# Decoder block on one core: gate slabs of the attention re-placed, statistics by quarters, merged tiles awaited one by one

## The chip, the cores and the metric

The kernel runs on one core of a Trainium2 chip. The metric is the time of the device for one execution, in microseconds. TensorE does the matmuls and the transposes, VectorE (DVE) and ScalarE (ACT) the element-wise work, GpSimd (POOL) the gathers, and SyncE (SP) issues most of the loads.

## The reference

One decoder layer on 512 tokens and 16 meta tokens of width 1024, in float32. Cut to the stages that the change touches:

```python
z = h @ w_in + b_in                      # q, k, v of both mixers, forget gate, gates ga and gb
oa = sliding_window_attention(...)       # 8 heads, window of 128, sinks, relative bias
ob = forgetting_attention(...)           # 8 heads, causal over all tokens, decayed
merged = sigmoid(ga) * (oa @ w_pa) + sigmoid(gb) * (ob @ w_pb)
y = merged @ w_o
h = layer_norm(DEEPNORM_ALPHA * h + y, ln1_g, ln1_b)
y = peer_ffn(h, ...)                     # top 16 of 16384 one-neuron experts for each of 8 heads
out = layer_norm(DEEPNORM_ALPHA * h + y, ln2_g, ln2_b)
```

## The kernel before

All large products are made slab by slab. A slab is 128 x 1024 numbers of a weight, eight tiles of 128 x 128. SyncE loads it into a ring of four (`load`), ScalarE rounds it to a high part (`split_hi`, L451), VectorE subtracts that and gets the low part (`split_lo`, L455), and TensorE makes of each tile three matmuls: high times low, low times high, high times high (`split_product`, L464 to L466). The splits run three slabs ahead of TensorE (`AHEAD`). With 512 tokens a tile is so three matmuls of 512 columns and a slab 24. Everything is float32 in parts, and each engine runs its own program in order; counters (semaphores) tie them together.

The stages, in order: 19 projection slabs; the attention, with gate slabs between; the `mix` slabs, one for each of the eight 128-row tiles m of the merged result; eight output slabs (`w_o`); the layer norm; 16 query slabs and the key scores; 128 slabs of `u_exp` and 128 of `v_exp`, beside which POOL gathers rows and VectorE uses them.

**The attention** has 64 units, a unit being one head of one block of 128 queries: 32 of the sliding window, in pairs, that is steps 0 to 15, and 32 of the forgetting attention, one a step, steps 16 to 47. Eight units are a block result; the blocks w = 0 to 7 end with steps 3, 7, 11, 15, 23, 31, 39 and 47. TensorE's iteration s issues the scores of step s + 1 (L1432), then the gate tiles that `TILES[s]` gives to this step, then the transposes of the probabilities of step s - 1 (L1453, L1456), then the products with the values of step s - 2 (L1475, L1478) into bank `psO[w % 2]`. VectorE adds bias and mask, takes the maximum (L942), inverts the sum and scales the probabilities `pexp` of step s - 1 (L951). ScalarE takes the exponentials (L614) and evacuates the transposes (L627, L630). Three iterations after a block ended, ScalarE takes its high part out of `psO` (`oT_hi`, L638) and VectorE, in the same iteration of its own loop, its low part (`oT_lo`, L960). The scores of step s stand in `psS[s % 2]`; in the last eight steps (40 to 47) a row has 528 columns, 16 of which lie in the second half, which else holds the result of the gate slabs.

**The gate slabs** are the columns ga and gb of `w_in`, two for each m. 14 of the 16 (`N_GATE`) are made in the attention, tile by tile as `TILES` says (16 steps of four tiles, 16 of two, then 3, 3, 2, 2, 2, 2, 2, 0, and none in the last eight steps), and ScalarE moves each result with its bias to `gate_input(v)` (L620). The two gates of m = 7 are made as whole slabs in the merge, ahead of the last `mix` slab.

**The merge.** For each m, TensorE makes the two products of `oT` into two of the banks 4 to 7, ScalarE has taken the sigmoid of the two gates (L648, L655), VectorE multiplies and adds (`mix`, L973, L975), and ScalarE and VectorE split the result (`m_hi` L658, `m_lo` L977). All three engines go in the same order of m.

**The output.** The eight output slabs start when all eight `m_lo` are there. VectorE makes `acc` from each (L995), and TensorE turns it behind the next slab (`turn_sum`, L1507) so that tokens are rows. Four of the turned tiles fill banks 4 to 7, 512 columns each; VectorE takes `bn_stats` of the four banks twice (`half_stats`, L984), after tile 3 and after tile 7, and the transposes of tile 4 wait for the first four. Behind the second four come `bn_aggr`, the inverse root, and a spread over the columns by small matmuls (L1527).

The lines that say what waits:

```python
                w = block_ended(s - 3)              # VectorE, attention
                if w is not None:
                    dve.wait_ge(o_hi_done, w + 1)
...
            pe.wait_ge(o_lo_done, 2 * NBLK)         # TensorE, ahead of the merge
...
                pe.wait_ge(m_lo_done, KT)           # TensorE, ahead of the output slabs
...
                if k == KT // 2:                    # TensorE, turn_sum
                    pe.wait_ge(r_stats_done, 1)
```

Of the kernel before, what the change touches and what calls it, by code (L numbers as in the profile page):

```python
# [21 lines left out]
P = 128  # L22
D = 1024
SEQ = 512
# [3 lines left out]
KT = D // P  # L28
# [20 lines left out]
N_GATE = 2 * (KT - 1)  # L49
FIRST_MIX = FIRST_MERGE + N_GATE  # L50
FIRST_OUT = FIRST_MERGE + N_MERGE
# [178 lines left out]

TILES = [4] * 16 + [2] * 16 + [3, 3, 2, 2, 2, 2, 2, 0] + [0] * 8

# [17 lines left out]
def build(nc, x, meta, consts, buckets, outside, norm_cols, b_cols, rel_bias, sinks, w_proj, w_merge, w_out,  # L250
          w_pq, subkeys, u_exp, v_exp, u_rows, norm_rows, out):
    ctx = ExitStack()
    with ctx:
# [53 lines left out]
        with ExitStack() as s:  # L307
            diag, unit_h = place(s, diag=([P, 2 * NBLK, P], F32), unit_h=([P, 2, SEQ], F32))
            stats1, mv1, rs1 = place(s, stats1=([P, NBLK, 12], F32), mv1=([P, NBLK, 2], F32), rs1=([P, 5, NBLK], F32))

# [50 lines left out]
        def out_bank(m):  # L361

            return (m + 4) % KT

        wide = [psS[:, 0, :], psS[:, 1, :], psT[:, :], psO[:, :, :].rearrange("p o q -> p (o q)")]
# [102 lines left out]
        def slab_parts(slot, k):  # L468
            return hi[:, slot, k * P:(k + 1) * P], lo[:, slot, k * P:(k + 1) * P]

        def gate_input(v):
# [102 lines left out]
        def _(act):  # L574
# [28 lines left out]
            for s in range(N_STEPS + 4):  # L603
# [13 lines left out]
                if v is not None:  # L617
                    act.wait_ge(slab_used, FIRST_MERGE + v + 1)
                    tile = N_PROJ + 8 * (v % 2) + v // 2
                    nc.scalar.activation(gate_input(v), psS[:, v % 2, SEQ:], ACT.Identity,  # L620
                                         bias=bcol[:, tile:tile + 1]).then_inc(gate_in_done, 1)
# [14 lines left out]
                if w is not None:  # L636
# [3 lines left out]
                                         ACT.Copy).then_inc(o_hi_done, 1)  # L640

            for m in range(KT):
                if m >= 2:
                    act.wait_ge(mix_done, m - 1)
                if m < KT - 1:
                    split_hi(act, FIRST_MIX + m + AHEAD)
                    for j in range(2):
                        nc.scalar.activation(gate[:, m % 2, j, :], gate_input(2 * m + j), ACT.Sigmoid).then_inc(gate_done, 1)  # L648
                else:
                    for j in range(3):  # L650
                        n = FIRST_MIX + m + j
                        split_hi(act, n + AHEAD)
                        if j < 2:
                            act.wait_ge(slab_used, n + 1)
                            nc.scalar.activation(gate[:, m % 2, j, :], psS[:, m % 2, j * SEQ:(j + 1) * SEQ], ACT.Sigmoid,  # L655
                                                 bias=bcol[:, N_PROJ + 8 * j + m:N_PROJ + 8 * j + m + 1]).then_inc(gate_done, 1)
                act.wait_ge(mix_done, m + 1)
                nc.scalar.activation(m_hi[:, m, :], mix[:, m % 2, 0, :], ACT.Copy).then_inc(m_hi_done, 1)  # L658
# [148 lines left out]
        def _(dve):  # L807
# [89 lines left out]
            dve.wait_ge(ck_in, 16)  # L897
            for s in range(N_STEPS + 4):
                last_step = 1 <= s <= N_STEPS
# [54 lines left out]
                if v is not None:  # L954
                    split_lo(dve, FIRST_MERGE + v + AHEAD)
                w = block_ended(s - 3)
                if w is not None:
# [4 lines left out]


            for m in range(KT):
                last = FIRST_MIX + m if m < KT - 1 else FIRST_OUT - 1
                for n in range(FIRST_MIX + m, last + 1):
                    split_lo(dve, n + AHEAD)
                dve.wait_ge(slab_used, last + 1)
                dve.wait_ge(gate_done, 2 * m + 2)
                if m >= 2:  # L970
                    dve.wait_ge(m_hi_done, m - 1)
                for j in range(2):
                    own.mark(V.tensor_tensor(mix[:, m % 2, j, :], banks[4 + 2 * (m % 2) + j], gate[:, m % 2, j, :], ALU.mult))  # L973
                own.settle()
                V.tensor_tensor(mix[:, m % 2, 0, :], mix[:, m % 2, 0, :], mix[:, m % 2, 1, :], ALU.add).then_inc(mix_done, 1)  # L975
                dve.wait_ge(m_hi_done, m + 1)
                V.tensor_tensor(m_lo[:, m, :], mix[:, m % 2, 0, :], m_hi[:, m, :].bitcast(F32),  # L977
                                ALU.subtract).then_inc(m_lo_done, 1)

            def half_stats(c):  # L980

                dve.wait_ge(r_turned, c + 1)
                for t in range(NBLK):
                    ins = V.bn_stats(stats1[:, t, 6 * c:6 * c + 6], banks[4 + t])  # L984
                    if t < NBLK - 1:
                        own.mark(ins)
                ins.then_inc(r_stats_done, 1)
                dve.wait_ge(r_stats_done, c + 1)

            for m in range(KT):  # L990
                split_lo(dve, FIRST_OUT + m + AHEAD)
                own.link(V.tensor_tensor(acc[:, m, :], hT_hi[:, m, 0:SEQ].bitcast(F32), hT_lo[:, m, 0:SEQ].bitcast(F32),
                                         ALU.add))
                dve.wait_ge(slab_used, FIRST_OUT + m + 1)
                V.scalar_tensor_tensor(acc[:, m, :], acc[:, m, :], ALPHA, psS[:, m % 2, 0:SEQ],  # L995
                                       ALU.mult, ALU.add).then_inc(r_done, 1)
                if m == KT // 2 + 1:
                    half_stats(0)
            half_stats(1)
            for t in range(NBLK):  # L1000
# [332 lines left out]
        def _(pe):  # L1333
# [85 lines left out]
            for s in range(-1, N_STEPS + 2):  # L1419
                r = s + 1  # L1420
                if r < N_STEPS:
                    if r >= 2:
                        pe.wait_ge(exp_done, exp_count(r - 2))
                    for u, first in placed(r):
                        window, n, h, tile, half = unit_of(u)
                        rows = slice(HD * half, HD * half + HD)
                        if width_of(u) > SEQ:
                            pe.wait_ge(gate_in_done, N_GATE - 1 + r % 2)
                        q = (qaT if window else qbT)[rows, tile, n * P:(n + 1) * P]
                        for c, k0, k1 in key_runs(u):  # L1430
                            k = kaT[rows, k0:k1] if window else kbT[rows, tile, k0:k1]
                            last = mm(psS[:, r % 2, first + c:first + c + k1 - k0], q, k, start=True, stop=True)  # L1432
                    last.then_inc(s_mm, 1)
                for done in range(tiles_before(max(s, 0)), tiles_before(s + 1)):
                    v, k = done // KT, done % KT
                    if k == 0:
                        pe.wait_ge(lo_done, FIRST_MERGE + v + 1)
                        if v >= 2:
                            pe.wait_ge(gate_in_done, v - 1)
                    last = slab(FIRST_MERGE + v, (FIRST_MERGE + v) % RING, psS[:, v % 2, SEQ:], tokens, tokens_lo,  # L1440
                                [(k, k)], ends=(k == 0, k == KT - 1))
# [17 lines left out]
                if s >= 2:  # L1459
# [20 lines left out]
                    last.then_inc(pv_mm, 1)  # L1480

            pe.wait_ge(o_lo_done, 2 * NBLK)
            for m in range(KT):
                for j in (range(3) if m == KT - 1 else (2,)):
                    n = FIRST_MIX + m + (j if m == KT - 1 else 0)
                    pe.wait_ge(lo_done, n + 1)
                    if j < 2:
                        last = slab(n, n % RING, psS[:, m % 2, j * SEQ:(j + 1) * SEQ], tokens, tokens_lo, all_k)
                    else:
                        if m >= 2:  # L1490
                            pe.wait_ge(mix_done, m - 1)
                        for e in range(2):
                            last = slab(n, n % RING, banks[4 + 2 * (m % 2) + e], lambda k: oT_hi[:, e, k, :],
                                        lambda k: oT_lo[:, e, k, :], [(4 * e + k, k) for k in range(4)])
                    last.then_inc(slab_used, 1)

# [3 lines left out]
            def turn_sum(k):  # L1500

                pe.wait_ge(r_done, k + 1)
                if k == KT // 2:
                    pe.wait_ge(r_stats_done, 1)
                for t in range(NBLK):
                    at = k % (KT // 2) * P
                    last = turn(banks[4 + t][:, at:at + P], acc[:, k, t * P:(t + 1) * P], ident)  # L1507
                if k % (KT // 2) == KT // 2 - 1:
                    last.then_inc(r_turned, 1)

            pe.wait_ge(gate_done, 2 * KT)
            for m in range(N_OUT):
                n = FIRST_OUT + m
                pe.wait_ge(lo_done, n + 1)
                pe.wait_ge(m_lo_done, KT)
                if m >= 2:
                    pe.wait_ge(r_done, m - 1)
                slab(n, n % RING, psS[:, m % 2, 0:SEQ], lambda k: m_hi[:, k, :], lambda k: m_lo[:, k, :],
                     all_k).then_inc(slab_used, 1)
                if m >= 1:  # L1520
# [211 lines left out]
```

## Time and profile before

| | us |
|---|---|
| median of 3 runs | 1705.8 |
| lowest and highest | 1704.66, 1707.39 |
| the profiled execution, its own time | 1718.52 |
| its span, first to last instruction | 1716.4 |
| TensorE busy | 1653.8 |
| VectorE busy | 1339.5 |
| ScalarE busy | 735.2 |
| GpSimd busy | 452.1 |
| mean granted clock of TensorE | 0.983 |

The profile comes from one execution, whose own time stands beside its span; the runs of the median were made without it. Times in the profile count from the first instruction. The attention lies between 149 and 360 us, the merge follows up to 417, the output slabs up to 478, and the two stages of expert slabs fill the time from 610 to 1700. A granted clock of 1.00 is TensorE's full 2.4 GHz and 0.50 is 1.2 GHz. Durations of single matmuls overlap each other, so it is the distance of their starts that tells the pace.

### The profile page before, as it was taken

The numbers are of one execution on the slowest core, as the hardware profiler recorded it, in microseconds if no ns is written. First come the engines' busy times: TensorE is split into PE (matmuls) and PEld (weight loads), VectorE is DVE, ScalarE is ACT, GpSimd is POOL, SyncE is SP. The second block draws the span as 40 slices with busy tenths as digits, with TensorE's granted clock in tenths as the row PEclk, the third lists the DMA queues.
The fourth block names the chain that finished last, engine by engine and source line by source line (L and its number), as shares of the span: only waits on it lengthen the run. The fifth ranks groups of instructions, "written<-read, shape, count | busy, mean of one in ns | idle before, by whom it ended". The sixth has DMA issues, their size and how long they took to land. (4 is left out here: it accounts for less than half of the span.)

```text
span 1716.4 us, 26821 instructions
## 1 busy us (share of the span) xinstructions
PE 1653.8 (96%) x9808; PEld 1523.3 (89%) x9808; DVE 1339.5 (78%) x2848; ACT 735.2 (43%) x1288; POOL 452.1 (26%) x314
## 2 busy tenths in 40 slices
PE   5999999999979999999999999999999999999996
PEld 4897776577768899999999999999999999999996
DVE  5434554644467888999999989967989999999898
ACT  4214544333143354566766754434333333333331
POOL 0000000000001105133132432332544545457550
PEclk9999999889989999999999999999999999999998
DMA  5731111012214459699899999999999999999991
GB/s 167 198 95 55 39 48 38 25 49 86 74 61 155 129 157 379 217 341 336 269 316 340 353 307 332 341 398 392 382 400 410 407 408 408 407 402 409 407 404 78
DMA packets 185441, 438.47 MB, mean 255 GB/s; under 512 B 17832, under 2 KB 102000, under 8 KB 182880
## 3 DMA queue, kind: packets, MB, share of 16 engines
q1 hardware_dynamic: 73872, 227.43, 36.3%
q0 software_dynamic: 44080, 161.06, 25.5%
q10 hardware_dynamic: 67360, 48.28, 8.5%
q8 instruction: 78, 1.28, 0.3%
q14 instruction: 51, 0.42, 0.1%
HBM read 380.57 MB, written 56.13 MB: 254 GB/s over the span
## 5 line engine op out<-in xcount | busy, mean ns | idle before, releaser
L464 PE MATMUL psS<-hT_lo,hi 128*128 128x368 f32 (+2 forms) x1504 | 518.4, 345 | 4.6 <-DVE hT_lo L1021 3.9
L465 PE MATMUL psS<-hT_hi,lo 128*128 128x368 f32 (+2 forms) x1504 | 510.1, 339 | 0.0
L466 PE MATMUL psS<-hT_hi,hi 128*128 128x368 f32 (+2 forms) x1504 | 508.5, 338 | 0.0
L455 DVE TENSOR_TENSOR lo<-raw,hi 128x1024 fp32r<-128x1024 f32 x323 | 394.6, 1222 | 119.7 <-ACT hi L451 110.5
L451 ACT ACTIVATE hi<-raw 128x1024 fp32r<-128x1024 f32 x323 | 340.0, 1053 | 177.4 <-PE psS L466 124.0
L569 POOL DMA_INDIRECT gat<-in_u_rows,idx x144 | 214.7, 1491 | 393.1 <-DVE gat L1195 214.8
L464 PEld LDWEIGHTS psS<-hT_lo,hi 128*128 128x128 f32 x1504 | 283.8, 189 | 30.8 <-issue 15.6
L466 PEld LDWEIGHTS psS<-hT_hi,hi 128*128 128x128 f32 x1504 | 283.9, 189 | 13.4
L465 PEld LDWEIGHTS psS<-hT_hi,lo 128*128 128x128 f32 x1504 | 283.8, 189 | 11.1
L569 POOL DMA_INDIRECT gat<-in_v_exp,idx x144 | 220.8, 1533 | 233.9 <-DVE gat L1195 151.4
L766 ACT ACTIVATE act_hi<-act_t 128x368 fp32r<-128x368 f32 x128 | 65.6, 513 | 278.9 <-DVE act_t L1246 264.0
L464 PE MATMUL psS<-act_lo,hi 128*128 128x368 f32 x512 | 169.6, 331 | 0.0
L465 PE MATMUL psS<-act_hi,lo 128*128 128x368 f32 x512 | 169.4, 331 | 0.0
L466 PE MATMUL psS<-act_hi,hi 128*128 128x368 f32 x512 | 168.9, 330 | 0.0
L1205 DVE SCALAR_TENSOR_TENSOR y_row<-gat,coef,y_row 128x1024 f32<-128x1024 f32 x128 | 164.0, 1281 | 2.6 <-DVE y_row L1205 0.5
L1195 DVE SCALAR_TENSOR_TENSOR gat<-gat,h_row 128x1024 f32<-128x1024 f32 x128 | 154.5, 1217 | 1.7 <-DMA gat<-in_u_rows,idx 1.7
L771 ACT ACTIVATE gelu<-psS 128x368 f32<-128x368 f32 x128 | 61.0, 476 | 185.5 <-PE psS L466 174.0
L556 POOL DMA_DIRECT2D sk_raw<-in_subkeys x1 | 0.5, 538 | 402.7 <-DVE acc L995 402.7
L465 PEld LDWEIGHTS psS<-act_hi,lo 128*128 128x128 f32 x512 | 96.2, 188 | 0.0
L466 PEld LDWEIGHTS psS<-act_hi,hi 128*128 128x128 f32 x512 | 96.2, 188 | 0.0
L464 PEld LDWEIGHTS psS<-act_lo,hi 128*128 128x128 f32 x512 | 96.1, 188 | 0.0
L464 PE MATMUL psT<-act_lo,hi 128*128 128x368 f32 x256 | 86.0, 336 | 3.4 <-DVE act_lo L1254 2.9
(303 smaller groups left out, 2630.1 us busy)
## 6 DMA issues: line engine op xcount, KB each, us to landing
raw<-in_u_exp SPq DMA_DIRECT2D x128, 512.0 KB
raw<-in_v_exp SPq DMA_DIRECT2D x128, 512.0 KB
gelu_dram<-gelu ACTq DMA_DIRECT2D x128, 184.0 KB
gates_dram<-gates ACTq DMA_DIRECT2D x92, 256.0 KB
gel_in<-gelu_dram SPq DMA_DIRECT2D x128, 184.0 KB
raw<-in_w_merge SPq DMA_DIRECT2D x24, 512.0 KB
gate_even<-gates_dram SPq DMA_DIRECT2D x8, 1472.0 KB
gate_odd<-gates_dram SPq DMA_DIRECT2D x8, 1472.0 KB
```

Source lines behind the costliest of these rows:

```text
L451: nc.scalar.activation(hi[:, n % RING, :], raw[:, n % RING, :], ACT.Copy).then_inc(hi_done, 1)
L455: nc.vector.tensor_tensor(lo[:, n % RING, :], raw[:, n % RING, :], hi[:, n % RING, :].bitcast(F32), ALU.subtract).then_inc(lo_done, 1)
L464: nc.tensor.matmul(out_ap, w_h, x_l, start=start, stop=False)
L465: nc.tensor.matmul(out_ap, w_l, x_h, start=False, stop=False)
L466: return nc.tensor.matmul(out_ap, w_h, x_h, start=False, stop=stop)
L556: pool.dma_start(sk_raw[:, :, :], subkeys).then_inc(keys_in, 16)
L569: nc.gpsimd.indirect_dma_start(out=gat[:, i % GATHERS, :], out_offset=None, in_=u_rows if kind == DOT else v_rows, in_offset=bass.Indirect ...
L766: nc.scalar.activation(act_hi[:, w % RING, :], act_t[:, w % RING, :], ACT.Copy).then_inc(ahi_done, 1)
L771: nc.scalar.activation(gelu[:, s % RING, :], banks[s % RING][:, 0:DENSE], ACT.Gelu).then_inc(gelu_done, 1)
L1195: V.scalar_tensor_tensor(row, row, 1.0, against, ALU.mult, ALU.mult, accum_out=dots[:, j:j + 1]).then_inc(item_done, 1)
L1205: V.scalar_tensor_tensor(total[:, :], row, coef[:, j:j + 1], total[:, :], ALU.mult, ALU.add).then_inc(item_done, 1)
```

## The change

- The splits and orders of the slabs change: all 16 gate slabs come first, then the eight `mix` slabs (`FIRST_MIX`, `w_merge`).
- `TILES`: steps 14 and 15 have three tiles instead of four, steps 32 to 39 have 2, 2, 2, 2, 1, 1, 0, 0, steps 40 to 43 none, and steps 44 to 47 two each. Slab 13 is made in these last four, in bank `psO[0]` (`gate_bank`), after a wait for the `oT_hi` and `oT_lo` of block 6, whose bank it is.
- VectorE's `oT_lo` comes four iterations after the block's end, not three; its loop is one longer.
- The gate slabs 14 and 15 (m = 7) are made as whole slabs directly behind the last attention step, into the two halves of `psS[1]`, ahead of the wait for the last `oT_lo`. ScalarE takes their sigmoids in the turn of m = 7. ScalarE and VectorE split two more slabs ahead of their loops over m.
- The first output slab waits for `m_lo` tile by tile.
- The statistics of the sums are taken by quarters: two turned tiles each, 256 columns, in banks 4 and 5, 6 and 7, 1 and 3, and 4 and 5 again (`sum_bank`); `stats1` is twice as long; VectorE takes a quarter ahead of its wait for the next output slab.

```diff
-FIRST_MIX = FIRST_MERGE + N_GATE
+FIRST_MIX = FIRST_MERGE + 2 * KT
-TILES = [4] * 16 + [2] * 16 + [3, 3, 2, 2, 2, 2, 2, 0] + [0] * 8
+TILES = [4] * 14 + [3] * 2 + [2] * 16 + [2, 2, 2, 2, 1, 1, 0, 0] + [0, 0, 0, 0, 2, 2, 2, 2]
+        def sum_bank(c, t):
+            return banks[((4, 5), (6, 7), (1, 3), (4, 5))[c][t // 2]]
+        def gate_bank(v):
+            return psS[:, v % 2, SEQ:] if v < N_GATE - 1 else psO[:, 0, :]
# ScalarE
+            for j in range(2):
+                split_hi(act, FIRST_MERGE + N_GATE + j + AHEAD)
             for m in range(KT):
                 if m >= 2:
                     act.wait_ge(mix_done, m - 1)
+                split_hi(act, FIRST_MIX + m + AHEAD)
+                for j in range(2):
+                    if m < KT - 1:
                         nc.scalar.activation(gate[:, m % 2, j, :], gate_input(2 * m + j), ACT.Sigmoid).then_inc(gate_done, 1)
+                    else:
+                        act.wait_ge(slab_used, FIRST_MERGE + N_GATE + j + 1)
+                        nc.scalar.activation(gate[:, m % 2, j, :], psS[:, 1, j * SEQ:(j + 1) * SEQ], ACT.Sigmoid,
...
# VectorE
-            for s in range(N_STEPS + 4):
+            for s in range(N_STEPS + 5):
-                w = block_ended(s - 3)
+                w = block_ended(s - 4)
+            for j in range(2):
+                split_lo(dve, FIRST_MERGE + N_GATE + j + AHEAD)
             for m in range(KT):
+                split_lo(dve, FIRST_MIX + m + AHEAD)
+                dve.wait_ge(slab_used, FIRST_MIX + m + 1)
...
+            def quarter_stats(c):
                 dve.wait_ge(r_turned, c + 1)
                 for t in range(NBLK):
+                    ins = V.bn_stats(stats1[:, t, 6 * c:6 * c + 6],
+                                     sum_bank(c, t)[:, t % 2 * (SEQ // 2):(t % 2 + 1) * (SEQ // 2)])
...
+                if m >= 3 and m % 2 == 1:
+                    quarter_stats((m - 3) // 2)
                 dve.wait_ge(slab_used, FIRST_OUT + m + 1)
                 V.scalar_tensor_tensor(acc[:, m, :], acc[:, m, :], ALPHA, psS[:, m % 2, 0:SEQ],
                                        ALU.mult, ALU.add).then_inc(r_done, 1)
-                if m == KT // 2 + 1:
-                    half_stats(0)
-            half_stats(1)
+            quarter_stats(3)
+            dve.wait_ge(r_stats_done, 4)
# TensorE
-                            pe.wait_ge(gate_in_done, N_GATE - 1 + r % 2)
+                            pe.wait_ge(gate_in_done, N_GATE - 1 - r % 2)
+                        if v == N_GATE - 1:
+                            pe.wait_ge(o_hi_done, 2 * NBLK - 1)
+                            pe.wait_ge(o_lo_done, 2 * NBLK - 1)
+            for j in range(2):
+                n = FIRST_MERGE + N_GATE + j
+                pe.wait_ge(lo_done, n + 1)
+                slab(n, n % RING, psS[:, 1, j * SEQ:(j + 1) * SEQ], tokens, tokens_lo, all_k).then_inc(slab_used, 1)
             pe.wait_ge(o_lo_done, 2 * NBLK)
             for m in range(KT):
+                n = FIRST_MIX + m
+                pe.wait_ge(lo_done, n + 1)
+                if m == 1:
+                    pe.wait_ge(gate_in_done, N_GATE)
...
-                if k == KT // 2:
+                if k == KT - 2:
                     pe.wait_ge(r_stats_done, 1)
                 for t in range(NBLK):
-                    at = k % (KT // 2) * P
-                    last = turn(banks[4 + t][:, at:at + P], acc[:, k, t * P:(t + 1) * P], ident)
-                if k % (KT // 2) == KT // 2 - 1:
+                    at = (t % 2 * 2 + k % 2) * P
+                    last = turn(sum_bank(k // 2, t)[:, at:at + P], acc[:, k, t * P:(t + 1) * P], ident)
+                if k % 2 == 1:
                     last.then_inc(r_turned, 1)
...
-                pe.wait_ge(m_lo_done, KT)
+                for k in range(KT):
+                    if m == 0:
+                        pe.wait_ge(m_lo_done, k + 1)
+                    last = slab(n, n % RING, psS[:, m % 2, 0:SEQ], lambda k: m_hi[:, k, :], lambda k: m_lo[:, k, :],
+                                [(k, k)], ends=(k == 0, k == KT - 1))
```

## Rows read from the trace of the kernel before

**Rows 1.** The page's first part: busy time of each engine.
```profile
PE 1653.8 (96%) x9808; PEld 1523.3 (89%) x9808; DVE 1339.5 (78%) x2848; ACT 735.2 (43%) x1288; POOL 452.1 (26%) x314
```

**Rows 2.** Waits of TensorE over the span: total us, times, longest us.
```profile
PE psS L464 <- DVE m_lo L977: 3.6, 1, 3.6
PE psT L1453 <- DVE pexp L951: 3.5, 4, 1.8
PE psT L1507 <- DVE stats L984: 3.3, 1, 3.3
...
PE psT L464 <- DVE oT_lo L960: 1.5, 1, 1.5
```

**Rows 3.** TensorE by stretches, late attention: length, busy us, granted clock, DMA, GB/s.
```profile
316.64:329.83 13.19, 13.19 (x73) 1.00 0.13 40
329.83:331.61 1.78, 0.00 (x1) 0.96 0.00 0
331.61:355.35 23.74, 23.74 (x82) 0.50 0.00 1
```

**Rows 4.** Timeline, iteration 42: start us, length us, instruction [idle before <-releaser].
```profile
327.97 0.57 ACT L638 ACTIVATE oT_hi<-psO 128x512 fp32r<-128x512 f32 x1
...
328.57 0.69 DVE L960 TENSOR_TENSOR oT_lo<-psO,oT_hi 128x512 fp32r<-128x512 f32 x1 [2.49 <-ACT oT_hi L638]
...
331.61 0.38 PE L1453 MATMUL psT<-cst,pexp 128*16 128x128 f32 x1 [1.78 <-DVE pexp L951]
```

**Rows 5.** Timeline, two tile-free steps at full clock.
```profile
319.51 1.25 PE L1432 MATMUL psS<-kbT,qbT 64*128 64x512 f32 x4
...
322.40 1.25 PE L1432 MATMUL psS<-kbT,qbT 64*128 64x512 f32 x4
...
323.69 0.78 DVE L934 SCALAR_TENSOR_TENSOR psS<-psS,cq,ckB 128x528 f32<-128x528 f32 x1 [0.51 <-PE psS L1432]
```

**Rows 6.** Timeline, end of the last `mix` slab: first and last of 15 matmuls.
```profile
413.61 0.40 PE L464 MATMUL psO<-oT_lo,hi 128*128 128x512 f32 x1
...
416.88 0.40 PE L466 MATMUL psO<-oT_hi,hi 128*128 128x512 f32 x1
```

**Rows 7.** TensorE by stretches around three waits behind the merge, columns as before.
```profile
417.28:420.86 3.58, 0.00 (x0) 0.91 0.07 30
420.86:427.24 6.38, 6.38 (x15) 0.52 0.25 85
459.21:462.55 3.34, 0.00 (x1) 0.79 0.00 0
462.55:468.31 5.76, 5.76 (x16) 0.53 0.23 91
...
492.09:495.49 3.40, 3.40 (x8) 0.53 0.00 0
```

**Rows 8.** VectorE: timeline rows, and groups by shape (busy us, mean ns | idle).
```profile
400.57 1.29 DVE L973 TENSOR_TENSOR mix<-psT,gate 128x512 f32<-128x512 f32 x2 [0.71 <-PE psT L466]
...
403.29 0.69 DVE L977 TENSOR_TENSOR m_lo<-mix,m_hi 128x512 fp32r<-128x512 f32 x1 [0.70 <-ACT m_hi L658]
...
480.05 1.28 DVE L984 BATCH_NORM_STATS2 stats<-psO 128x6 f32<-128x512 f32 x2
...
L455 DVE TENSOR_TENSOR lo<-raw,hi 128x1024 fp32r<-128x1024 f32 x12 | 14.7, 1225 | 14.8 <-ACT hi L451 14.7
...
L942 DVE TENSOR_REDUCE nmax<-psS 128x1 f32<-128x528 f32 x8 | 5.7, 708 | 0.3
...
L942 DVE TENSOR_REDUCE nmax<-psS 128x1 f32<-128x400 f32 x8 | 4.6, 574 | 0.3
```

**Rows 9.** ScalarE, timeline at the start of the merge.
```profile
360.08 1.05 ACT L451 ACTIVATE hi<-raw 128x1024 fp32r<-128x1024 f32 x1
361.15 1.28 ACT L648 ACT_TABLE_LOAD   x1
362.44 1.15 ACT L648 ACTIVATE gate<-early_gates 128x512 f32<-128x512 f32 x2
```

More of the change, by code:

```diff
@@ L308, in build @@
             diag, unit_h = place(s, diag=([P, 2 * NBLK, P], F32), unit_h=([P, 2, SEQ], F32))
-            stats1, mv1, rs1 = place(s, stats1=([P, NBLK, 12], F32), mv1=([P, NBLK, 2], F32), rs1=([P, 5, NBLK], F32))
+            stats1, mv1, rs1 = place(s, stats1=([P, NBLK, 24], F32), mv1=([P, NBLK, 2], F32), rs1=([P, 5, NBLK], F32))
         with ExitStack() as s:
@@ L619, in _ @@
                     tile = N_PROJ + 8 * (v % 2) + v // 2
-                    nc.scalar.activation(gate_input(v), psS[:, v % 2, SEQ:], ACT.Identity,
+                    nc.scalar.activation(gate_input(v), gate_bank(v), ACT.Identity,
                                          bias=bcol[:, tile:tile + 1]).then_inc(gate_in_done, 1)
@@ L644, in _ @@
                     act.wait_ge(mix_done, m - 1)
-                if m < KT - 1:
-                    split_hi(act, FIRST_MIX + m + AHEAD)
-                    for j in range(2):
+                split_hi(act, FIRST_MIX + m + AHEAD)
+                for j in range(2):
+                    if m < KT - 1:
                         nc.scalar.activation(gate[:, m % 2, j, :], gate_input(2 * m + j), ACT.Sigmoid).then_inc(gate_done, 1)
[L649 to L656, printed above, removed]
+                    else:
+                        act.wait_ge(slab_used, FIRST_MERGE + N_GATE + j + 1)
+                        nc.scalar.activation(gate[:, m % 2, j, :], psS[:, 1, j * SEQ:(j + 1) * SEQ], ACT.Sigmoid,
+                                             bias=bcol[:, N_PROJ + 8 * j + m:N_PROJ + 8 * j + m + 1]).then_inc(gate_done, 1)
                 act.wait_ge(mix_done, m + 1)
@@ L961, in _ @@
                                     oT_hi[:, w // NBLK, :, cols].bitcast(F32), ALU.subtract).then_inc(o_lo_done, 1)
+            for j in range(2):
+                split_lo(dve, FIRST_MERGE + N_GATE + j + AHEAD)
             for m in range(KT):
[L965 to L968, printed above, removed]
+                split_lo(dve, FIRST_MIX + m + AHEAD)
+                dve.wait_ge(slab_used, FIRST_MIX + m + 1)
                 dve.wait_ge(gate_done, 2 * m + 2)
@@ L978, in _ @@
                                 ALU.subtract).then_inc(m_lo_done, 1)
-            def half_stats(c):
+            def quarter_stats(c):
                 dve.wait_ge(r_turned, c + 1)
                 for t in range(NBLK):
-                    ins = V.bn_stats(stats1[:, t, 6 * c:6 * c + 6], banks[4 + t])
+                    ins = V.bn_stats(stats1[:, t, 6 * c:6 * c + 6],
+                                     sum_bank(c, t)[:, t % 2 * (SEQ // 2):(t % 2 + 1) * (SEQ // 2)])
                     if t < NBLK - 1:
@@ L987, in half_stats @@
                 ins.then_inc(r_stats_done, 1)
-                dve.wait_ge(r_stats_done, c + 1)
             for m in range(KT):
@@ L1439, in _ @@
                             pe.wait_ge(gate_in_done, v - 1)
-                    last = slab(FIRST_MERGE + v, (FIRST_MERGE + v) % RING, psS[:, v % 2, SEQ:], tokens, tokens_lo,
+                        if v == N_GATE - 1:
+                            pe.wait_ge(o_hi_done, 2 * NBLK - 1)
+                            pe.wait_ge(o_lo_done, 2 * NBLK - 1)
+                    last = slab(FIRST_MERGE + v, (FIRST_MERGE + v) % RING, gate_bank(v), tokens, tokens_lo,
                                 [(k, k)], ends=(k == 0, k == KT - 1))
@@ L1480, in _ @@
                     last.then_inc(pv_mm, 1)
+            for j in range(2):
+                n = FIRST_MERGE + N_GATE + j
+                pe.wait_ge(lo_done, n + 1)
+                slab(n, n % RING, psS[:, 1, j * SEQ:(j + 1) * SEQ], tokens, tokens_lo, all_k).then_inc(slab_used, 1)
             pe.wait_ge(o_lo_done, 2 * NBLK)
             for m in range(KT):
[L1484 to L1495, printed above, removed]
+                n = FIRST_MIX + m
+                pe.wait_ge(lo_done, n + 1)
+                if m == 1:
+                    pe.wait_ge(gate_in_done, N_GATE)
+                if m >= 2:
+                    pe.wait_ge(mix_done, m - 1)
+                for e in range(2):
+                    last = slab(n, n % RING, banks[4 + 2 * (m % 2) + e], lambda k: oT_hi[:, e, k, :],
+                                lambda k: oT_lo[:, e, k, :], [(4 * e + k, k) for k in range(4)])
+                last.then_inc(slab_used, 1)
             pe.wait_ge(ones_set, 1)
@@ L1514, in _ @@
                 pe.wait_ge(lo_done, n + 1)
-                pe.wait_ge(m_lo_done, KT)
                 if m >= 2:
                     pe.wait_ge(r_done, m - 1)
-                slab(n, n % RING, psS[:, m % 2, 0:SEQ], lambda k: m_hi[:, k, :], lambda k: m_lo[:, k, :],
-                     all_k).then_inc(slab_used, 1)
+                for k in range(KT):
[3 more added lines that the diff above has]
+                                [(k, k)], ends=(k == 0, k == KT - 1))
+                last.then_inc(slab_used, 1)
                 if m >= 1:
@@ L1703 @@
                                      tiles(a["w_pb"][0])], axis=2)], axis=1)
-    w_merge = np.concatenate([both[:-1, :2].reshape(N_GATE, P, D), both[:-1, 2].reshape(KT - 1, P, D),
-                              both[-1].reshape(3, P, D)])
+    w_merge = np.concatenate([both[:, :2].reshape(2 * KT, P, D), both[:, 2].reshape(KT, P, D)])
     bias = a["b_in"][0]
```

## The prediction

> **What bounds the kernel now.** The page first: TensorE is busy for 96% of the span [rows 1], so time can only come from the few places where it waits or runs at its lower clock. The waits of TensorE, longest first, then say where [rows 2]. After the start-up wait the list holds four that the change touches: four waits for a normalised `pexp` tile in the attention (3.5 us together, the longest 1.8), one for the last `oT_lo` (1.5), one for the last `m_lo` (3.6), and one for the first statistics of the sums (3.3). The granted clock, stretch by stretch, shows what these waits drag behind them. In the attention TensorE ran 13.19 us of steps without gate tiles at 1.00, then waited 1.78 us, and then ran 23.74 us, all busy, at 0.50, the lower of its two levels (1.2 of 2.4 GHz) [rows 3]. In the output projection each of the two waits is followed by some 6 us of which most is at 0.50 [rows 7]. The pace confirms it: at 1.00 the 512-column matmuls start 0.2336 us apart (14 steps from 413.61 to 416.88) [rows 6]; behind the first of these waits 15 of them take 6.38 us, 0.43 each [rows 7].
>
> **Why the clock fell in the attention.** At iteration 42 ScalarE splits block 6 (`oT_hi`, at 327.97) and VectorE, in the same iteration, stands at the head of its queue waiting for that; its `oT_lo` starts at 328.57 and only then come the bias, the maximum and the normalised `pexp` for which TensorE waits until 331.61 [rows 4]. Without that a tile-free step takes 322.40 - 319.51 = 2.89 us and VectorE idles 0.51 us in it [rows 5]: TensorE sets the pace, VectorE is close behind.
>
> **The change, part by part.** The matmuls stay the same in number and shape; only their places move. What moves no time: the reordered slabs in DRAM (same bytes, same order of loads, each still three slabs ahead of its use), the waits for `m_lo` in eight pieces (waits alone), the `bn_stats` in 16 halves (below).
>
> (1) `oT_lo` one iteration later. ScalarE's half is done by then, so VectorE doesn't stand: the four waits go, 3.5 us [rows 2]. The 0.69 us of work stays. In iteration 43, a tile-free one, it exceeds the 0.51 of idle by 0.2; TensorE's transpose comes after its 1.25 us of scores [rows 5], so I take this as hidden. Who is late next: a slab now ends at step 37, its `lo` split of 1.22 us [rows 8] comes in iteration 38, also tile-free. 1.22 - 0.51 = 0.7 late, of which TensorE's scores cover a part: I take a new wait of 0.3, between 0 and 0.7.
>
> (2) The low clock of 23.74 us in the attention. If it doesn't fall, half of that, 11.9 us, comes back. Tile-free steps go from nine (39 to 47) to six (38 to 43); steps 44 to 47 get two tiles each (6 matmuls, 1.4 us at that pace). The tiles in steps 32 to 37 thin out from 16 to 10, and two tiles leave steps 14 and 15; those only move. Does it fall? For: six tile-free steps are 17 us, and in the trace 13.19 us of them ran at 1.00 until the 1.78 us wait. Against: once low, the same steps kept it low though TensorE never stood. The upper bound of the gain is 11.9, the lower a loss (rivals). I take 11.9, as the only thing that stood between the 13.19 us at 1.00 and the fall is the wait that part 1 removes. The Trainium skill ("TensorE: Matmul & The Clock Gate", Part 4: PE-mode transpose) says that transposes on TensorE do not count as busy for the clock in the same way as matmuls. By that rule tile-free steps, with five transposes each, would lose the clock without any wait, and the sum would be 17 instead of 29; the 13.19 us at 1.00 speak against it, the 23.74 us at 0.50 for it.
>
> (3) The last gate slab in bank `psO[0]`. Its first tile waits for `oT_lo` of block 6 (iteration 43 of VectorE), and behind it stand transposes 43. But scores 45, ahead of it in the queue, need `exp` 43, which is about as late, and then last 1.25 us: cost 0. Its evacuation on ScalarE comes in iteration 48, before `mix` tile 1 needs the bank over 15 us later: 0.
>
> (4) Two gate slabs (11.2 us) directly behind the last attention step. Their splits were done in the attention. They cover `oT_hi`, `oT_lo`: the 1.5 us go. ScalarE has two more slab splits ahead of the sigmoids of m = 0; it gets to these when the second gate slab ends, and split, table load and two sigmoids are 1.05 + 1.28 + 1.15 = 3.5 us [rows 9] of the 5.6 (24 matmuls) that the first `mix` slab takes: 0. The sigmoids of m = 7 read both halves of `psS[1]`; output slab 0 is in `psS[0]`, and they run within `mix` slab 7.
>
> (5) Merged tiles one by one. `m_lo` of tile 6 starts 2.7 us after the products that follow its slab (403.29 against 400.57) and takes 0.69 [rows 8], so it is there within `mix` slab 7. Tile 7 comes 3.6 us after slab 7; seven tiles of three matmuls are 4.9 us. The wait of 3.6 goes, and with it the fall of the clock: 15 matmuls took 6.38 us where 15 x 0.2336 + 0.1 = 3.6 do, 2.8 more [rows 7]. Together 6.4.
>
> (6) Statistics by quarters. Transposes of a second half need no bank that is still being read: quarter 3 reuses the banks of quarter 0, read four slabs earlier. The wait of 3.34 goes. After it four transposes and 12 matmuls took 5.76 [rows 7] where 0.4 (an estimate for the transposes) + 2.8 + 0.1 = 3.3 do: 2.5 more. Together 5.8. VectorE gets 4 halves a slab, some 1.4 us, in a slab of 6 us of which it has over 2 free (a split, a sum and an accumulation are 2.6). At the end four `bn_stats` of 512 columns (1.28 for two) become four of 256. The maxima of 400 and 528 columns differ by 0.134 us, 1.05 ns a column [rows 8], so 256 columns less are 0.27 each, 1.07 for four, less 0.05 for 48 more elements in the aggregates at that pace: 1.0.
>
> (7) The small matmuls behind the statistics and the first query slabs start after waits that stay, at 0.50. The first query matmuls lost least of all: 3.40 us at 0.53, some 1.6 lost, where the two other restarts lost 2.8 and 2.5 [rows 7]. Where the clock comes back shifts with the moments of the waits, so I take the mean of the three, 2.3: 0.7 more.
>
> Sum: 3.5 + 11.9 + 1.5 + 6.4 + 5.8 + 1.0 - 0.3 - 0.7 = 29.1 us. Everything behind the statistics (1200 us of matmuls at 1.00) only moves forward. The profiled execution took 1718.5 (span 1716.4), and would take 1689.4. The three unprofiled runs have a median of 1705.8, 12.7 less; I subtract the same sum: **1676.7 us**.
>
> **The rivals.** (A) The clock falls in the tile-free steps all the same, or the 12.7 us between profile and median are just these 11.9, that is, the unprofiled runs never had the low stretch. For the first: page and trace above, and the new 0.3 us wait. For the second: the sizes agree. Against it: the three runs lie within 2.7 us, and a chance fall would spread them by 12. Either leaves 17.2 us: 1688.6. Fallen at step 43 and not raised by the tiles of 44 to 47 it would be 1676.7 + 2.9 + 12.9 + 3.1 + 3.3 = 1698.9. (B) Slower than before: the thinned steps 36 to 38 and the split in 38 pull the clock down at step 39, and two tiles in 4.3 us don't lift it. At full clock the rest is 5 x 2.9 (39 to 43) + 3 x 4.3 (44 to 46) + 3.05 (47, without scores) + 3.3 (48, 49) = 33.8 us, which would be lost once more: 1710.5. It decides if the fall comes by step 40 (30.9 lost, over 29.1); from step 41 on (28.0) it doesn't. For: tile-free work at 0.50 stayed there for 23.74 us. Against: 13.19 us at 1.00 just before. (C) A new wait in the moved part: ScalarE, with two more splits ahead of the first sigmoids, has them some 3 us late, after the cover of 5.6; the first products and `mix` slab 2 wait, and the clock falls once (2.8): 5.8 back, 1682.5. (D) `oT_lo` one iteration later still finds `oT_hi` late and nothing changes in the attention: 29.1 - 15.4 = 13.7, 1692.1. The trace has ScalarE's split done 3 us before iteration 43 of VectorE gets there.
>
> **How the numbers follow.** Forecast 0.74, A 0.13, C 0.06, D 0.03, B 0.04. The forecast's own range is 1672 to 1682: 2 for the unknown restarts, 1 for the new wait, the rest for profile against median. With A and C the range reaches 1690, which leaves out less than 2 in 10. A measurement of this kernel can tell about 0.2% (3.4 us) from no change. All cases but B are over that faster: faster 0.95, same 0.01, slower 0.04.
>
> **What would show it.** In the changed kernel's profile: granted clock 1.00 from the start of the attention to the last transposes of the sums; no wait for `pexp` over 0.5 us (a 0.3 one near step 39); none for `oT_lo`, `m_lo` or `stats`; mixed tiles and output slabs without a gap; four `bn_stats` at the end at 0.33 us pace; PE busy time down by some 17 us, since low-clock work counts longer. Wrong would be: any stretch at 0.50 within steps 36 to 49, a wait at the first tile of the last gate slab, or at the first `mix` slab.

## The result and the profile after

The changed kernel takes 1690.3 us (median of 4 runs, 1688.6 to 1692.5) against 1705.6 before (4 runs, 1704.7 to 1707.4): a ratio of 0.991, 95% interval 0.9893 to 0.9927. It is faster, by 15.3 us where 29.1 were forecast, and 0.3 us outside the range. The two profiled executions differ by more: 1718.5 before and 1688.6 after, 29.9 less, nearly the forecast. (The one profiled after is the fastest of its four runs; against their median the difference is 28.2.) The prediction broke where it carried the sum of the profile over to the median of the other runs.

In the profile every step that was forecast is there. The waits of TensorE up to the start of the query slabs, without those of the kernel's start-up (us in total, times, longest):

```profile
PE psS L1542 <- DVE diag L1017: 4.8, 1, 4.8
PE psS L468 <- DVE hT_lo L1028: 3.9, 1, 3.9
PE psS L1404 <- DVE vT L887: 0.9, 1, 0.9
PE psS L1439 <- ACT vM L609: 0.8, 1, 0.8
PE psT L1519 <- DVE acc L1003: 0.3, 1, 0.3
```

TensorE's busy time is 1637.6 us, 16.2 less, where some 17 were forecast. Of the four groups of waits in [rows 2] none is left, and no new one came: not at the last gate slab, not in iteration 39, not at the first `mix` slab. The same stretches of TensorE as in [rows 3, 7], now in the kernel after (length, busy us, records, granted clock, DMA, GB/s):

```profile
330.00:344.25 14.25, 14.25 (x91) 1.00 0.04 10
344.25:355.41 11.16, 11.16 (x49) 1.00 0.37 129
355.41:400.20 44.79, 44.79 (x193) 1.00 0.26 83
400.20:449.20 49.00, 48.66 (x225) 1.00 0.28 97
449.20:453.97 4.77, 0.00 (x0) 0.89 0.64 220
453.97:457.75 3.78, 3.78 (x16) 0.50 0.00 0
```

These are the late attention (to 344.25), the two gate slabs behind it, the `mix` slabs and the output slabs, with gaps of 0.34 us in all and at 1.00; the clock first falls in the wait for `diag`, which the change leaves in place. The `oT_lo` of block 6, the last but one, now stands where VectorE had room (start us, length us):

```profile
320.01 0.48 DVE L957 TENSOR_SCALAR pexp<-pexp,rsum 128x528 f32<-128x528 f32 x1
320.41 0.68 DVE L966 TENSOR_TENSOR oT_lo<-psO,oT_hi 128x512 fp32r<-128x512 f32 x1
321.31 0.78 DVE L940 SCALAR_TENSOR_TENSOR psS<-psS,cq,ckB 128x528 f32<-128x528 f32 x1 [0.21 <-PE psS L1439]
```

VectorE still idles 0.21 us behind it, where [rows 5] show 0.51 without it. At the end of the output slabs the statistics stand as

```profile
449.24 1.43 DVE L990 BATCH_NORM_STATS2 stats<-psT 128x6 f32<-128x256 f32 x4 [0.75 <-PE psT L1519]
450.70 0.63 DVE L1008 BATCH_NORM_AGGREGATE mv<-stats 128x2 f32<-128x24 f32 x4
```

against two groups like the 1.28 us of [rows 8] and, in the kernel before,

```profile
481.36 0.43 DVE L1001 BATCH_NORM_AGGREGATE mv<-stats 128x2 f32<-128x12 f32 x4
```

### The profile page after: what moved, and what is told of

It is laid out like the page before. It is cut to its first block and busy times, and to the rows that moved or that the text cites. A ratio compares the mean times of both kernels' runs of the same rounds, so it can differ in the third digit from the quotient of the medians.

```text
span 1686.4 us, 26830 instructions
## 1 busy us (share of the span) xinstructions
PE 1637.6 (97%) x9808; PEld 1513.4 (90%) x9808; DVE 1341.2 (80%) x2856; ACT 734.1 (44%) x1288; POOL 454.0 (27%) x314
## 3 DMA queue, kind: packets, MB, share of 16 engines
q8 instruction: 78, 1.28, 0.3%
## 5 line engine op out<-in xcount | busy, mean ns | idle before, releaser
L469 PEld LDWEIGHTS psS<-hT_hi,lo 128*128 128x128 f32 x1496 | 282.8, 189 | 10.8
```

What stands on the lines that cost most here:

```text
L469: nc.tensor.matmul(out_ap, w_l, x_h, start=False, stop=False)
```

## Experiments

Each run has its mean granted clock on record. The runs of the kernel before fall into two groups: 0.987 to 0.991 and at most 1709.5 us, or 0.981 to 0.985 and at least 1715.1 us, with none between. The profile of [rows 3] and those of the two kernels with a longer wait, below, have the low stretch of 24 us in the attention and 0.983 or 0.984; the profiles without it have 0.989 or more. So I count a run at 0.985 or less as one with this long stretch. Shorter falls of the clock, a few microseconds long, can't be counted this way. A median "without" leaves the runs with the long stretch out.

**The kernel before, again.** The edit is none.

> The kernel before, unchanged, run again. T1 (the low stretch of 23.7 us in the late attention is an accident of the one profiled execution; the other runs of the kernel before don't have it): the runs lie at 1705.6 with a mean granted clock of about 0.990, and a new profile most likely shows TensorE at 1.00 through steps 36 to 49, with the 1.78 us wait still there. T2 (the low stretch is in every run, and a profile adds some 13 us): clock 0.983 in all runs, and a low stretch of some 20 us again in the new profile.

1707.2 us, ratio 1.0001 (0.9972 to 1.0029). Three of its 12 runs are at 0.983 and 1717.9 to 1719.3, nine at 0.990 or 0.991 and 1705.5 to 1707.7. Beside the experiments and in this one the kernel before ran 98 times on four chips: 31 runs with the low stretch (median 1717.9), 67 without (1706.7). By chip these are 9 of 47, 8 of 23, 9 of 17 and 5 of 11; chance alone would spread four such shares as far about one time in twenty, so a difference between chips is possible and not shown. The new profile is one without:

```profile
316.09:329.28 13.19, 13.19 (x73) 1.00 0.12 40
329.28:331.06 1.78, 0.01 (x1) 1.00 0.00 0
331.06:348.70 17.64, 17.17 (x112) 1.00 0.01 1
```

The steps and the wait of 1.78 us are the same, to the hundredth, as in [rows 3]; behind the wait the clock stays at 1.00, and the rest of the attention takes 17.64 us, a new wait of 0.46 us in it, where it took 27.95 (331.61 to 359.56). So the stretch cost 10.8 us and not the half of 23.74: a tile-free step took 5.92 us at 0.50 (335.29 to 341.21) and takes 3.20 at 1.00 (333.08 to 336.28). The medians of the runs with and without it differ by 11.2. T1 holds: the profile that the prediction was made from showed something that less than a third of the runs have. T2 falls: the profiled execution took 1707.15 us and lies among the others.

**Only `oT_lo` later.**

```diff
-            for s in range(N_STEPS + 4):
+            for s in range(N_STEPS + 5):
-                w = block_ended(s - 3)
+                w = block_ended(s - 4)
```

> Only VectorE's oT_lo moved one iteration later. T1: the four waits for pexp go and nothing else, 3.5 us faster than before (1702). T2: the clock no longer falls either, 15.4 us faster (1690).

1702.8 us, ratio 0.9954 (0.9931 to 0.9978): 3.9 under the 1706.7 of the runs without the long stretch, and none of its 12 runs has it (all 0.989 to 0.992). In its profile one wait for `pexp` of 0.5 us is left, and all nine tile-free steps are there at 1.00. So the waits went and their length was gained. That the long stretch went with them fits, but beside 9 of 47 on this chip twelve runs without one come up by chance one time in thirteen.

**Only the `m_lo` waits one by one.**

```diff
-                pe.wait_ge(m_lo_done, KT)
...
+                for k in range(KT):
+                    if m == 0:
+                        pe.wait_ge(m_lo_done, k + 1)
...
```

> Only the m_lo waits one by one. Both theories: the wait of 3.6 us and the restart at low clock (2.8 in the profile, 1.7 to 3 by where the restart falls) go, 5.3 to 6.6 us faster (1699.0 to 1700.3). A rival, that output slab 0 waits inside for its last tile: about 1 us less.

1702.7 us, ratio 0.9954 (0.9931 to 0.9977): 4.0 less, not 5.3 to 6.6. The wait is gone, and output slab 0 runs through at 1.00:

```profile
402.90:408.90 6.00, 6.00 (x27) 1.00 0.33 101
408.90:414.60 5.70, 5.70 (x26) 1.00 0.07 25
```

So the rival (a wait inside the slab) is out. What is missing of the gain was lost in other places: its profile has two short stretches at 0.50 that the profile of the kernel before, run again, hasn't, one behind the wait of 1.78 us in the attention and one behind the wait for the first statistics:

```profile
330.21:331.99 1.78, 0.01 (x1) 1.00 0.00 0
331.99:335.59 3.60, 3.60 (x16) 0.53 0.00 0
335.59:351.21 15.62, 15.15 (x98) 1.00 0.01 2
448.10:451.60 3.50, 3.50 (x10) 0.51 0.50 149
```

The first cost 1.6 us (19.22 from the end of the wait to that of the attention, against 17.64), and the second about as much. With these 3.2 off, the 3.6 of the wait and 2.9 of its restart leave 3.3; the two profiled executions differ by 3.1 (1707.15 and 1704.01). Three of the 12 timed runs, at 1699.3 to 1700.4 and 0.991, have the whole forecast gain, most others some 3 us less; one of these, at 0.985 and 1706.6, counts as a run with the long stretch. The first of the two short stretches ended within tile-free steps: the clock can come back in these.

**Only the statistics by quarters.** The edit is `quarter_stats`, `sum_bank` and `turn_sum` as in the change.

> Only the statistics by quarters. Both theories: the wait of 3.3 us, its restart (2.5) and 1.0 at the end go, 6.8 us faster (1698.8). Rival: the restart behind the later wait costs more, as the clock is full until then: some 5.5 us.

1702.0 us, ratio 0.9964 (0.9939 to 0.999). Three of 12 runs, at 1709.7 to 1712.1 and 0.984 or 0.985, have the low stretch, as the wait for `pexp` is still there; the other nine have a median of 1701.5, 5.2 less than before. The rival's 5.5 is near, its reason isn't seen: around the start of the query slabs this profile has 3.4 us at 0.50, that of the kernel before, run again, 6.9. That profile says why the restart is worth less than 2.5: there the wait of 3.35 us for the statistics and the work behind it passed without a fall.

```profile
448.15:451.50 3.35, 0.01 (x1) 1.00 0.00 0
451.50:457.30 5.80, 5.80 (x27) 1.00 0.23 90
```

Seven profiles have this wait: in three the clock stayed at 1.00 (that of the kernel before, run again, the one with only `oT_lo` later, the one with the wait of 2.5 us below), in three it was at 0.50 for 3.4 us, in that of [rows 7] for 6.9.

**Only the slabs.** The changed kernel with the other three parts undone.

> Only the slabs' part: TILES, the last gate slab in psO[0] and two gate slabs behind the last step; oT_lo as before (three iterations), m_lo awaited whole, statistics by halves. T1: the wait for the last oT_lo goes (1.5 us) and nothing of the rest; the wait for pexp in iteration 43 stays, and as it comes in tile-free steps it brings the low clock in some runs. 1704.5 to 1706, at most 3 us faster than before. Rival: the low stretch is short now, since tiles in steps 44 to 47 raise the clock again: no run over 1712.

1705.1 us, ratio 0.9968 (0.9946 to 0.999): 1.5 less than the runs of before without the long stretch, the length of the wait for the last `oT_lo`. No run is over 1709.5 or under 0.987, though four waits for `pexp` (2.6 us, the longest 1.8) are in its profile, which is at 1.00 throughout the attention. That speaks for the rival in this expectation, for which the next run has a profile.

**The changed kernel with `oT_lo` early again.**

```diff
-            for s in range(N_STEPS + 5):
+            for s in range(N_STEPS + 4):
-                w = block_ended(s - 4)
+                w = block_ended(s - 3)
```

> The changed kernel with VectorE's oT_lo back in the iteration of ScalarE's oT_hi. T1: the waits for pexp come back, 3 to 3.5 us slower than the changed kernel (1693.5), and one run in five falls to the low clock, 5 to 12 us longer. If the thinner tiles kept the clock up by themselves, no run would be at 0.985 or lower.

1695.8 us (6 runs, 1693.6 to 1696.5), ratio 0.991 (0.9881 to 0.994); the changed kernel has 1690.0 (16 runs). Its profile, TensorE by stretches around the wait in iteration 43:

```profile
323.15:324.93 1.78, 0.01 (x2) 1.00 0.00 0
324.93:326.75 1.82, 1.82 (x15) 1.00 0.00 0
326.75:333.60 6.85, 6.85 (x20) 0.50 0.01 2
333.60:351.11 17.51, 17.51 (x107) 1.00 0.05 7
```

Behind the wait of 1.77 us (to 324.93) the clock falls at 326.7, 1.8 us after the wait ended; the first gate tiles of step 44 run from 329.3, and at 333.6 it is back. The low stretch is 6.9 us instead of 23.9 and costs at most 3.4; with waits of 2.9 (2.6 and one of 0.3) that is some 6, beside the 5.8 us measured. Five of its six runs are at 0.989 or 0.990 and one, the fastest, at 0.992, so the fall seems frequent here. None of the 18 runs of this kernel and the one above, which have the wait and the new tiles, has the long stretch, where 8 of 23 of the kernel before on the same chip have it: the new places of the tiles shorten the fall. They don't prevent it.

**The changed kernel, again, twice.**

> The changed kernel, unchanged, run again beside the kernel before. T1 (the low stretch is a matter of chance in the kernel before, some 1 run in 5, and gone in the changed one): all runs between 1688 and 1693 at a mean clock of 0.992, median 1690.3; 17 us under the median of before. Rival: the changed kernel has rare slow runs of its own, 5 to 12 us longer at 0.985, from its six tile-free steps.

> The changed kernel beside the one with filled waits, on the same chip. T1: 1689.5 to 1690.5, mean clock 0.992 or 0.993, no run over 1693; in the kernel before, again, some runs at 0.983 and 1716 or more.

1689.9 us (ratio 0.9877, 0.9848 to 0.9906) and 1690.0 (0.9864, 0.9825 to 0.9903). With the first four these are 16 runs on several chips, 1687.6 to 1692.5, all at 0.991 to 0.994: no long stretch, and none in the attention of the three profiles. 1690.0 is 16.6 under the 1706.7 of before without it, 27.9 under the 1717.9 with it. Over all profiles: of the eight with the long wait in the attention five have a fall of the clock behind it, of the six without (the changed kernel, that with only `oT_lo` later, and the filled ones below) none. The rival with rare slow executions of its own isn't borne out.

**A longer wait in the kernel before.** The `oT_lo` of block 6 is computed twice, and in another kernel four times, with the same result.

```diff
+                    if w == 6:
+                        for _ in range(3):
+                            own.link(V.tensor_tensor(oT_lo[:, w // NBLK, :, cols], psO[:, w % 2, :].rearrange("p (t q) -> p t q", t=4),
+                                                     oT_hi[:, w // NBLK, :, cols].bitcast(F32), ALU.subtract))
```

> The kernel before with the oT_lo of block 6 computed twice in iteration 42, which makes the 1.78 us wait of TensorE some 2.6 us long. The other blocks as before. T1 (the wait is what lets the clock fall, by how it meets the chip's own rhythm): the low stretch comes in clearly more than 1 run in 5, half or more at 0.983 and 1718 to 1721. If the wait had nothing to do with it, the share stays at 1 in 5 and all runs are 0.8 longer.

> The kernel before with the oT_lo of block 6 computed four times in iteration 42, so that TensorE's wait of 1.78 us becomes some 4 us. T1 (it is the wait that lets the clock fall, and a longer one meets it more surely): nearly all runs have the low stretch, 0.983, 1719 to 1722. If the fall had another cause, the share stays at 1 in 4 and the others lie at 1709.

The waits became 2.5 and 4.0 us. Twice: 1709.8 us, 1.0006 (0.9981 to 1.0031), four of 12 runs at 1716.7 or more and 0.983 to 0.985, beside 8 of 23 of the kernel before on the same chip: no higher share. Four times: 1717.9 us, 1.0028 (0.9998 to 1.0058), nine of 12, beside 9 of 17 on the same chip. Against the 31 of 98 of all chips nine of 12 is more, against the 9 of 17 beside it the sample can't say. A wait of 4 us isn't sure to bring the long stretch either: three runs are at 0.989 or 0.990. Without the wait none of 28 runs has it, but how its length sets the share stays open. The profile of the kernel with four, around the end of the wait at 334.23:

```profile
329.80:333.90 4.10, 0.47 (x3) 0.79 0.00 0
333.90:356.00 22.10, 21.77 (x74) 0.50 0.00 1
```

**The changed kernel with its last two waits filled.** Small matmuls of constants into bank 0, which nobody reads then; their results are not used.

```diff
+            def fill(count):
+                for i in range(count):
+                    mm(banks[0][:, i % NBLK * P:(i % NBLK + 1) * P], ones[:, :], ident, start=True, stop=True)
+            fill(18)
             for part, (done, bank) in enumerate(((diag_done, 1), (shift_done, 3))):
...
                 last.then_inc(spread_done, 1)
+            fill(14)
```

> The changed kernel with 18 small matmuls of ones by the unit matrix into a free bank in the 4.8 us wait for diag, and 14 in the 3.9 us wait behind the spread; their results are not used. T1 (the lower clock of the restarts is worth what the profile shows: 13.7 us low there, 8.7 of them busy): the clock stays at 1.00, the spread's matmuls take 1.8 instead of 3.8 us and the query slabs start at full pace, 3.5 to 4.5 us faster than the changed kernel (1685.5 to 1686.5). Rival: the small matmuls don't hold the clock, and then they end late, 3 us slower (1693).

> The kernel with filled waits again. If its 2.7 us over the changed kernel were not the chip's, it is 2 to 3 us faster here too (1687.3). Rival: no difference beyond 1 us, the 2.7 us came from another chip.

1687.2 us twice (ratios 0.9868, 0.9832 to 0.9904, and 0.985, 0.981 to 0.9889); the second time the changed kernel ran on the same chip, with 1690.0, 2.8 more. It beats both kernels. The profile of the first:

```profile
450.22:454.40 4.18, 4.18 (x38) 1.00 0.75 247
454.40:455.15 0.75, 0.01 (x1) 1.00 0.06 22
455.15:457.20 2.05, 2.05 (x18) 1.00 0.03 8
457.20:460.33 3.13, 3.13 (x29) 1.00 0.00 0
460.33:461.08 0.75, 0.01 (x2) 1.00 0.00 0
461.08:466.00 4.92, 4.92 (x21) 1.00 0.00 0
```

The sixteen matmul records of the spread take 2.05 us where the changed kernel needs 3.78, and the query slabs start at full pace, where the changed kernel has 4.8 us at 0.50:

```profile
457.75:461.66 3.91, 0.04 (x2) 0.50 0.00 0
461.66:466.44 4.78, 4.78 (x11) 0.50 0.00 0
```

The first twelve matmuls of the query slabs take 5.1 us there and 2.8 here, so the profiles have 1.7 + 2.3 = 4.0 us; the median gained 2.8. Six of the 12 runs are at 0.996 or 0.997 (1685.3 to 1687.1), six at 0.994 or 0.995 (1687.2 to 1690.6). Both profiled executions are of the second kind, and in both the clock was low elsewhere: at the start of the kernel in the first (first line), and at 573 us, where the profile of the changed kernel has it too, and at 669 us, at the end of a wait of 2.6 us for VectorE's `best`, in the second.

```profile
25.40:35.70 10.30, 9.77 (x39) 0.50 0.43 120
573.10:576.60 3.50, 3.42 (x11) 0.51 0.48 146
668.75:672.20 3.45, 3.37 (x12) 0.51 0.79 209
```

## Why the prediction was wrong

**The step that failed** is part (2), the 11.9 us for the low clock in the attention, as it was carried over to the runs of the median ("I subtract the same sum"). The profile of before was one of the executions with the low stretch; the three runs of the median were not. In its place the second profile shows an attention at 1.00 throughout, and the mean clock of 67 of 98 runs of the kernel before leaves no room for the long stretch. Without the term the sum is 17.2 us and the time 1688.6, 1.7 from the measured one; that was half of rival A, at 0.13. The two sizes that agreed, 12.7 between profile and median and 11.9 of low clock, should have weighed more. The term was also sized too large for the executions that have the stretch: 10.8 us by the two profiles, since a step took 5.92 us at 0.50 and 3.20 at 1.00, not half. The argument that stood against it (three runs within 2.7 us, where chance would spread them by 12) was weak: at 31 of 98 three runs without the stretch come up one time in three.

Between the two profiled executions the sum held, 29.1 forecast and 29.9 found, in part by luck: another execution of the kernel before loses another amount behind the same waits, as the seven profiles with the wait for the statistics show. Point by point, I compare the distances between marks in the profile of the kernel before without the long stretch (the second profile) and in the one after. The marks are the end of the last value product (348.70 and 344.25), of the last `mix` slab (406.40 and 400.37), the first output slab (409.98 and 400.20), the last transpose of the sums (465.25 and 449.20) and the first `diag` matmul (470.89 and 453.97):

(1) 4.5 us up to the end of the attention, forecast 3.2: the wait of 0.3 didn't come, and the second profile has a fifth wait of 0.46 that went too. These are 4.0; the other 0.5 wasn't traced. Alone: 3.9.

(2) The clock stayed at 1.00 in the tile-free steps of all three profiles of the changed kernel, and none of its 16 runs has the long stretch: right as a mechanism. The run with `oT_lo` early again ties it to the removed wait: that edit alone brought the fall back. The new places of the tiles are a second guard: they shorten a fall. (The prediction counts 16 tiles in steps 32 to 37 before; that is the number of steps 32 to 38, steps 32 to 37 have 14. Nothing in the sum hangs on it.) The page's rule on transposes (the Trainium skill, "TensorE: Matmul & The Clock Gate", Part 4: PE-mode transpose) would, as the prediction reads it, have the tile-free steps lose the clock without a wait. Nine of them were at 1.00 in the profile with `oT_lo` alone later, and none of the 28 runs without the long wait has the long stretch, so it isn't borne out here. Once the clock is low, it can come back in these steps or not: in three profiles they ran at 0.50 for 23.9 us (23.74 of them in [rows 3]), in the one with only the `m_lo` waits changed it was back after 3.4. What decides stays open.

(3) and (4) cost nothing, as forecast; the 1.5 us of `oT_lo` went (1.6 by the marks, 1.5 alone).

(5) 3.75 us for the wait by the marks, and 2.9 more in the output slabs for the restart (5.8 busy us at 0.50), forecast 3.6 and 2.8. In the timed runs of that part alone only 4.0 of 6.4 came; in its profile the rest went in two short falls elsewhere.

(6) 3.3 us for the wait by the marks (6.27 less the 2.9 of the first restart), and nothing for its restart, which that profile doesn't have. In the timed runs the part gave 5.2, with the end of the statistics. The size was off here: the forecast took both restarts as certain, and they are not. The end: four `bn_stats` of 256 columns take 1.43 us and save 1.07, as forecast; the aggregate of 24 columns takes 0.63 instead of some 0.43, 0.2 more and not 0.05, so 0.86 instead of 1.0.

(7) The last restart is at 0.50 for 4.8 busy us; twelve matmuls took 5.1 us where 2.8 do, 2.3 lost, the mean of three that was taken.

The four parts alone give 3.9 + 4.0 + 5.2 + 1.5 = 14.6 us of the 16.6 together. The 2 us between them may be restarts, since after a wait taken away the next one can meet a fall that was not there before, as in the profile with only the `m_lo` waits changed; that isn't shown.

Rival B (slower, a fall by step 40) is out: no run of the changed kernel is slower or has the fall. Rivals C and D are excluded by the waits of the profile after.

## What to carry to other kernels

Before a stretch at the lower clock is priced, ask whether it is in the timed runs: where the profiled execution is longer than their median by just the loss that its low stretch explains, take the stretch as absent from the median until a second profile says otherwise. A restart at the lower clock is not a certain cost either: price it by how often it is seen. A short wait of TensorE between attention steps without gate tiles was worth its length in the median (3.9 us), and more in the mean over runs: 31 of 98 times 11.2 us, an estimate of 3.5 us on top. It was removed by moving the one instruction that waited at the head of VectorE's queue one step later. Where a wait couldn't be removed, matmuls of constants into a free bank held the clock at 1.00 through it in both profiles: 2.8 us for two waits of 4.8 and 3.9.

## What the runs showed of the hardware that had not been expected

The same wait of 1.78 us, after the same 13.19 us of work, had three different sequels in profiles of the same attention: 23.9 us at 0.50, 3.4 us at 0.50, and none. By the mean clock 31 of 98 executions have the long stretch and 67 don't. In the changed kernel with `oT_lo` early the fall came 1.8 us after the wait had ended, when TensorE was busy again. The wait of 3.35 us for the first statistics, between dense output slabs, passed at 1.00 in three of seven profiles, and the one of 3.6 us for `m_lo` in one of seven (that of the slabs alone); in [rows 7] both were followed by some 6 us of which most were at 0.50.
